# Two post-norm scale columns turned into rows: through a line of DRAM instead of diagonals on TensorE

## The reference, cut to what matters

```python
c_act = silu(c)
mod = c_act @ ada_w + ada_b                      # 6 vectors of 2048
sh1, sc1, g1, sh2, sc2, g2 = split(mod, 6)
u = rms_norm(x, mix_norm_pre) * (1 + sc1) + sh1
y = token_mixer(u)                               # retention and MoBA branches, gated, merged, @ w_out
x = x + (1 + g1) * rms_norm(y, mix_norm_post)    # first scale row
u = rms_norm(x, ffn_norm_pre) * (1 + sc2) + sh2
y = conv_ffn(u)                                  # @ w_up, causal conv, silu gate, @ w_down
x = x + (1 + g2) * rms_norm(y, ffn_norm_post)    # second scale row
```

## Time and profile before

| what | value |
|---|---|
| runs of the kernel | 1826.56, 1824.75, 1826.43 us (median 1826.43) |
| the profiled execution | 1826.54 us, span in the profile 1824.5 us |
| PE busy | 1804.5 us (99%) |
| VectorE busy | 1369.1 us (75%) |
| ScalarE busy | 859.4 us (47%) |
| granted TensorE clock | 0.997 of full speed |
| chain that ended last | PE 95%, DMA 2%, DVE 2%, ACT 1% |

### The profile page before, as it was taken

One profiled execution on the slowest core, in us unless ns is written; L12 is line 12 of the kernel. 1 busy time (PEld: TensorE's weight loads), 2 busy tenths in 40 slices (PEclk: granted clock), 3 DMA queues, 4 the chain that ended last, 5 costly groups with the idle time before them and its releaser, 6 DMA issues.

```text
span 1824.5 us, 26219 instructions
## 1 busy us (share of the span) xinstructions
PE 1804.5 (99%) x8989; PEld 1532.7 (84%) x8989; DVE 1369.1 (75%) x1968; ACT 859.4 (47%) x994; POOL 192.1 (11%) x271
## 2 busy tenths in 40 slices
PE   8999999999999999999999999999999999999998
PEld 6788888888888888888888888888888888888886
DVE  6887788878888788888997577777777776744555
ACT  4444544444454535463445455444444444444444
POOL 0000122222222222222210000000000000000000
PEclk9999999999999999999999999999999999999999
DMA  9999688878888888979886636556555555555552
GB/s 354 387 387 353 196 270 266 290 238 271 270 262 273 262 281 242 292 235 303 279 269 216 212 125 199 185 187 193 193 186 184 186 192 193 187 187 201 187 194 106
DMA packets 304739, 432.96 MB, mean 237 GB/s; under 512 B 50740, under 2 KB 174308, under 8 KB 304032
## 3 DMA queue, kind: packets, MB, share of 16 engines
q1 hardware_dynamic: 244160, 360.25, 59.7%
q0 software_dynamic: 20736, 67.34, 10.6%
q10 hardware_dynamic: 39776, 4.49, 1.8%
HBM read 429.79 MB, written 2.23 MB: 237 GB/s over the span
## 4 chain that ended last, share of the span: by engine, by line
PE 95%; DMA 2%; DVE 2%; ACT 1%; SPq 0%; issue 0%; DVEq 0%; ACTq 0%
PE ps L957 18%; PE ps L580 12%; PE ps L578 12%; PE ps L579 12%; PE ps L609 10%; PE ps L965 9%; PE ps L1026 4%; PE ps L1024 4%; PE ps L1025 4%; PE ps L711 1%; PE ps L713 1%; PE ps L712 1%; DMA ada_first<-in_ada_w 1%; PE ps L617 1%; DMA stage<-in_w_in 1%; DVE ada_acc L1600 1%
## 5 line engine op out<-in xcount | busy, mean ns | idle before, releaser
L1502 DVE TENSOR_TENSOR w_low<-stage,w_high 128x1024 fp32r<-128x1024 f32 x608 | 743.2, 1223 | 379.5 <-ACT w_high L1070 361.9
L1070 ACT ACTIVATE w_high<-stage 128x1024 fp32r<-128x1024 f32 x552 | 583.9, 1060 | 724.1 <-PE ps L580 274.0
L578 PE MATMUL ps<-w_high,lhs 128*128 128x512 f32 x992 | 389.4, 393 | 0.9 <-issue 0.9
L580 PE MATMUL ps<-w_high,lhs 128*128 128x512 f32 x992 | 386.3, 389 | 0.0
L579 PE MATMUL ps<-w_low,lhs 128*128 128x512 f32 x992 | 386.1, 389 | 0.0
L957 PE MATMUL ps<-lhs,w_high 128*128 128x512 f32 x1408 | 336.7, 391 | 0.0
L957 PEld LDWEIGHTS ps<-lhs,w_high 128*128 128x128 f32 x1408 | 258.5, 188 | 50.1 <-issue 0.2
L558 POOL DMA_DIRECT2D ada_ring<-in_ada_w x256 | 185.0, 723 | 753.8 <-DVE ada_acc L1526 544.4
L1526 DVE SCALAR_TENSOR_TENSOR ada_acc<-ada_ring,c_act,ada_acc 128x256 f32<-128x256 f32 x480 | 230.6, 480 | 20.9 <-DMA ada_ring<-in_ada_w 11.0
L578 PEld LDWEIGHTS ps<-w_high,lhs 128*128 128x128 f32 x992 | 186.2, 188 | 39.5 <-issue 1.3
L580 PEld LDWEIGHTS ps<-w_high,lhs 128*128 128x128 f32 x992 | 186.2, 188 | 39.0
(11 more groups left out here) (218 smaller groups left out, 1541.9 us busy)
## 6 DMA issues: line engine op xcount, KB each, us to landing
stage<-in_w_in SPq DMA_DIRECT2D x100, 1024.0 KB, 6.9
stage<-in_ffn_w_up SPq DMA_DIRECT2D x176, 512.0 KB, 4.4
ada_ring<-in_ada_w POOLq DMA_DIRECT2D x256, 256.0 KB, 5.7
stage<-in_ffn_w_down SPq DMA_DIRECT2D x44, 1024.0 KB, 5.0
ada_first<-in_ada_w SPq DMA_DIRECT2D x64, 512.0 KB, 11.4
stage<-in_w_in SPq DMA_DIRECT2D x56, 512.0 KB, 11.5
stage<-in_ret_w_o SPq DMA_DIRECT2D x16, 1024.0 KB, 6.8
stage<-in_moba_w_o SPq DMA_DIRECT2D x16, 1024.0 KB, 7.4
```

The lines of the kernel that those rows point to most:

```text
L578: pe.matmul(acc, hi, w_high[:, slot, k, :], start=kt == 0, stop=False)
L580: last = pe.matmul(acc, lo, w_high[:, slot, k, :], start=False, stop=kt == KT - 1)
L1070: act.activation(w_high[:, h % 4, :, :], stage[:, slot, 2 * (h % 2):2 * (h % 2) + 2, :], ACT.Copy).then_inc(high_ready, 1)
L1502: dve.tensor_tensor(w_low[:, h % 4, :, :], stage[:, slot, 2 * (h % 2):2 * (h % 2) + 2, :], w_high[:, h % 4, :, :].bitcast(F32), ALU.subtra ...
```

## The change

Both vectors take the same way. VectorE still works out the column (`gain_sum`, then one half of `gain`, now 128 x 2 x 16); the high and low parts, the diagonals, the spreads and the copies out of PSUM are gone. ScalarE writes the column with a DMA to a line of DRAM in feature order (`gain_to_memory`: 128 x 16 pieces of 4 bytes) and later, behind a wait on that write, issues a load that reads the 8 KB line 128 times into `gain_b` (`gain_to_rows`, 1 MB). First vector: write behind part 6 of the first G_MOBAO group, load behind part 2 of the second. Second vector: write behind part 6 of the third G_OUT group, load behind part 0 of the second up group. The idle matmuls read `ones_r[:, 0:1]` with a step of zero instead of `diag2`. PE's waits on `gain_ready` and `gain_diag` go; where the second spread waited for the modulated halves, the next up group's first part now does.

```diff
             def keep_busy(times):
                 for _ in range(times):
-                    pe.matmul(ps[:, 0, :], ones_r[:, :], diag2[:, 0:NC], start=True, stop=True)
+                    pe.matmul(ps[:, 0, :], ones_r[:, :], ones_r[:, 0:1].broadcast_to([P, NC]), start=True, stop=True)
...
                         elif first:
-                            pe.wait_ge(gain_ready, 5)
+                            pe.wait_ge(u2_even, KT // 2)
+                            pe.wait_ge(u2_odd, KT // 2)
...
-                    if G_MOBAO <= G < G_OUT and h == 5:
-                        spread_gain(G - G_MOBAO)
...
-                    if first and parity == 0 and h == 6:
-                        pe.wait_ge(u2_even, KT // 2)
-                        pe.wait_ge(u2_odd, KT // 2)
-                        pe.wait_ge(gain_diag, 4 * KT)
-                        for n in range(4):
-                            last = spread(4 + n, diag2, n)
-                        last.then_inc(gain_spread, 1)
...
+            def gain_to_memory(which):
+                act.wait_ge(gain_col, 2 * which + 2)
+                act.dma_start(gain_line[int(which)].rearrange("(k p) -> p k", p=P), gain[:, int(which), :],
+                              allow_slow_non_contiguous=True).then_inc(gain_out, 16)
+            def gain_to_rows(which):
+                act.wait_ge(gain_out, 16 * which + 16)
+                act.dma_start(gain_b[:, :], gain_line[which:which + 1, :].broadcast_to([P, D])).then_inc(gain_ready, 16)
...
-                    if G_MOBAO < G <= G_OUT and h == 1:
-                        k = G - 1 - G_MOBAO
-                        act.wait_ge(gain_spread, k + 1)
-                        act.activation(gain_b[:, k * NC:(k + 1) * NC], ps[:, 6, :], ACT.Copy).then_inc(gain_ready, 1)
+                    if (G, h) in ((G_MOBAO, 6), (G_OUT + 2, 6)):
+                        gain_to_memory(G > G_MOBAO)
+                    if G == G_MOBAO + 1 and h == 2:
+                        act.wait_ge(lhs_ready, 8 * 2 + 8)
+                        gain_to_rows(0)
...
                 if h == 0:
-                    act.wait_ge(gain_spread, 5)
-                    act.activation(gain_b[:, :].rearrange("p (b n) -> p b n", b=4), ps[:, 4:8, :], ACT.Copy
-                                   ).then_inc(gain_ready, 1)
+                    act.wait_ge(y_gained, 8)
+                    gain_to_rows(1)
...
-                    if G_MOBAO <= G < G_OUT and h == 5:
-                        k = G - G_MOBAO
-                        wait(dve, gain_spread, k - 1)
-                        for i in range(4):
-                            diagonal(diag1, k % 2, i, 4 * k + i)
...
                     if G > G_OUT and h == 3:
-                        dve.wait_ge(gain_ready, G - G_OUT)
+                        dve.wait_ge(gain_ready, 16)
...
-                    if G > G_OUT and h == 5:
-                        if G == G_OUT + 1:
-                            dve.wait_ge(gain_spread, 4)
-                            gain_column(1)
-                        k = G - 1 - G_OUT
-                        for i in range(16 * k // 3, 16 * (k + 1) // 3):
-                            diagonal(diag2, i // 4, i % 4, i)
+                    if G == G_OUT + 1 and h == 5:
+                        gain_column(1)
...
-            dve.wait_ge(gain_ready, 5)
+            dve.wait_ge(gain_ready, 32)
```

More of the change, by code:

```diff
@@ L134, in hybrid_block @@
         shift2 = sb("shift2", [P, KT])
-        gain = sb("gain", [P, KT])
-        gain_high = sb("gain_high", [P, KT], F32R)
-        gain_low = sb("gain_low", [P, KT], F32R)
+        gain_sum = sb("gain_sum", [P, KT])
+        gain = sb("gain", [P, 2, KT])
         post_cols = sb("post_cols", [P, 4 * KT])
@@ L167, in hybrid_block @@
                [("v_ret", [P, T, 1024], F32), ("o_ret", [P, T, 1024], F32)],
-               [("src_b", [P, KT, SEQ], F32)],
-               [("below_diag1", [P, KT // 2, SEQ], F32), ("diag1", [P, 4 * NC], F32R)])
+               [("src_b", [P, KT, SEQ], F32)])
         region("hold_r", 4096, [("src_a", [P, KT, SEQ], F32)])
@@ L297, in hybrid_block @@
         gain_col = sem("gain_col")
-        gain_diag = sem("gain_diag")
-        gain_spread = sem("gain_spread")
+        gain_out = sem("gain_out")
         gain_ready = sem("gain_ready")
@@ L333, in hybrid_block @@
         ada_line = nc.dram_tensor("ada_line", (4, ADA_BG), F32, kind="Internal").ap()
+        gain_line = nc.dram_tensor("gain_line", (2, D), F32, kind="Internal").ap()
         block = ctx.enter_context(nc.Block())
@@ L1823, in gain_column @@
                 a = (0, 3 * KT)[which]
-                dve.scalar_tensor_tensor(out=gain[:, :], in0=ada_cols[:, a:a + KT], scalar=1.0,
+                dve.scalar_tensor_tensor(out=gain_sum[:, :], in0=ada_cols[:, a:a + KT], scalar=1.0,
                                          in1=post_cols[:, (2 + which) * KT:(3 + which) * KT], op0=ALU.add, op1=ALU.add
                                          ).then_inc(gain_col, 1)
-                dve.wait_ge(gain_col, 4 * which + 1)
-                dve.tensor_tensor(gain[:, :], gain[:, :], post_cols[:, which * KT:(which + 1) * KT], ALU.mult
+                dve.wait_ge(gain_col, 2 * which + 1)
+                dve.tensor_tensor(gain[:, which, :], gain_sum[:, :], post_cols[:, which * KT:(which + 1) * KT], ALU.mult
                                   ).then_inc(gain_col, 1)
-                dve.wait_ge(gain_col, 4 * which + 2)
-                dve.tensor_copy(gain_high[:, :], gain[:, :]).then_inc(gain_col, 1)
-                dve.wait_ge(gain_col, 4 * which + 3)
-                dve.tensor_tensor(gain_low[:, :], gain[:, :], gain_high[:, :].bitcast(F32), ALU.subtract
-                                  ).then_inc(gain_col, 1)
-                dve.wait_ge(gain_col, 4 * which + 4)
-            def diagonal(diag, n, i, tile):
-                for part, column in enumerate((gain_high, gain_low)):
-                    at = (2 * n + part) * NC + i * P
-                    dve.tensor_scalar(diag[:, at:at + P], ident[:, :], column[:, tile:tile + 1].bitcast(F32), None,
-                                      ALU.mult).then_inc(gain_diag, 1)
             for G in range(G_RETO, G_UP):
@@ L1975, in first_up_side @@
                     mean_of_rows(slice(0, T), 3, 1)
-                    dve.wait_ge(gain_ready, 4)
+                    dve.wait_ge(gain_ready, 16)
                     gain_y(3, 0, 1)
```

7 lines of the change are left out of this document (1 added, 6 removed).

## The result

The changed kernel took 1830.94 us (median of 8 runs, 1828.23 to 1833.84), the kernel before 1826.49 us (8 runs, 1824.75 to 1827.26). The ratio is 1.003 with a 95% interval of 1.0021 to 1.0038: slower by 0.3%, where 0.2% faster was forecast and the range ended at 1825.6 us. The profiled execution took 1830.11 us; its span is 3.6 us longer than before's, and the medians are 4.45 us apart.

The account below looks back on a forecast made before the run. PE was taken to bound the kernel, busy 1804.5 of 1824.5 us. Removed PE work of 2.08 + 1.85 = 3.93 us, all else 0, took the median 1826.43 to 1822.50 us; range 1820.9 to 1825.6 us.

Parts of the forecast that it names:

- the removed work on PE: Spread matmuls gone from PE: four pairs in the MoBA output product, 2.08 us, plus eight later, 1.85 us; 3.93 us less.
- the second row's block: Eight spread matmuls between parts 6 and 7 of the first up group; removing them saves PE 1.85 us.
- no price for the edits on VectorE and ScalarE: Diagonal writes and copies removed, DMA issues added; both engines run ahead of PE, so 0 us.
- the loads of the rows: 1 MB broadcast loads on ScalarE's queue, 3.5 us each at 301 GB/s, within PE's 4.7 us slack; cost 0.
- the idle matmuls: 28 in the handover to the up projection, reading with step zero; equal slots of 0.23 us assumed, cost 0.
- the moved waits: Waits for the modulated halves, moved to the next up group's head; already met by then, no PE wait.
- Rival 2: Handover: zero-step read doubles the idle matmuls' slots, 5.4 us in all; net +1.5, 1827.9 us; chance 0.05.
- rival 3: Removed slots come back: weight stream or ada ring late once, 1 MB load up to 3.5 us; net -0.4; chance 0.07.
- I take 9 us, the slowest such row, within the 17.2: First column's write of 2048 4-byte pieces lands in 9 us, as the slowest ada_quads read; cost 0.
- The upper bound of 36 us: Column write's latest landing, if all of the slowest read grows with the pieces: 4 x 9.0 us.
- rival 1: First column's write lands after 17.2 us, ScalarE's load wait delays PE; at 36 us net +14.9, 1841 us; chance 0.08.
- the budget of 17.2 us: Time for the first column's write to land before PE waits for a low part: from 904.2 to 921.4 us.

Follow-up runs that it names:

- Dense: Changed kernel with each column written to DRAM as 128 pieces of 64 bytes, rows in another number order; 1822.15 us, ratio 0.9981 to the kernel before.
- zerostep: Kernel before with only the 28 idle matmuls' operand changed to one column of ones read with step zero; 1826.71 us, ratio 1.0002.
- Block: Dense with ScalarE, before the first load of the rows, also waiting until PE has finished part 2 of that group; 1830.27 us, ratio 1.0023.
- lateload: Changed kernel with the first load of the rows, and ScalarE's wait for the write, one group later, write unmoved; 1825.88 us, ratio 0.9999.

## Why the prediction was wrong

**Right: the removed work on PE.** The sum was 3.93 us. Dense and before differ by 3.97; the periods of the transposes after are 22.65 and 22.66 us where 22.64 was written, and the second row's block is worth 1.84 (1.85). The reading of slots from a period, ripple included, held.

**Right: no price for the edits on VectorE and ScalarE, the loads of the rows, the idle matmuls and the moved waits.** Dense has all of these edits and gains the whole sum; zerostep has the operand alone and costs nothing; and PE's waits after show none for the moved waits. Rival 2 falls. Of rival 3 the 1 MB load falls; its other half, an ada ring that is late once, did come, but through the write.

**Wrong: "I take 9 us, the slowest such row, within the 17.2".** The step was the landing of the write, and it measured 19.8 us. The row it was taken from had reads of 4-byte cells and writes of 32 bytes. I treated both as like a 4-byte write, on the ground that 512 pieces land no later than 128. What decided was none of these: with the same 2048 pieces 64 bytes apart the write lands in 14.0 us, inside the budget, and side by side in 19.8. The upper bound of 36 us covered it, but rival 1 got a chance of 0.08, although the number of pieces, the queue and the nearly full DMA engines stood there as grounds; a net price of 5.9 to 14.9 us against a gain of 4 asked for more, and the range should have reached it.

**Wrong: the budget of 17.2 us.** I went from the waiting instruction to ScalarE's and VectorE's next parts, and from those to the PE part that uses them. But between part 2 and part 3 stand the transposes on PE, and they need gate_a, which VectorE does behind the low part of part 3. The trace of before holds it, between the low part of 918.67 and the transposes of 925.37:

```profile
920.20 1.27 DVE L1863 TENSOR_TENSOR gate_b<-gate_b,ps 128x512 f32<-128x512 f32 x2
921.51 1.23 DVE L1866 TENSOR_TENSOR gate_a<-gate_a,gate_b 128x1024 f32<-128x1024 f32 x1
```

By the chain above the way from ScalarE's release to the transposes takes 5.6 us (924.91 to 930.52), so the latest moment was 925.37 - 0.5 - 5.6 = 919.3, 15.1 us after the issue and not 17.2. With this budget the landing of 19.8 us costs 4.7 us, and 4.85 were measured; by mine it would be 2.6. Block, which was given such a wait without the small write, bears the path out.

**Not foreseen: two further ways.** The write slowed the traffic beside it, a price that the prediction put at nothing and that stands even when nobody waits for the landing (lateload, 3.7 us). And the waits of 3.7 and 5.7 us were followed by a spell at the lower clock (1.83 us after, 2.08 in block). Rival 1 was priced as a wait alone. The whole: 1822.5 + 4.85 + 1.83 = 1829.2 us, within the changed kernel's runs but 1.8 us under their median. These runs spread more than those of before (5.6 us against 2.5), and one trace does not show what the longer ones had in addition.

By the Trainium skill's DMA: Bandwidth & Descriptors (Specifications) a transfer under 512 B is a read-modify-write. That pointed at the right instruction. The prediction made 18 us of it against a budget of 17.2; it came to 19.8 against 15.1. But no run here shows a read-modify-write as such, and the pieces of 64 bytes in dense are under that size as well and land in 3.1 to 4.4 us, so a size under 512 B did not by itself make a write late here.

## What to carry to other kernels

Do not write a column to DRAM in 4-byte cells side by side beside a stream that has no slack: turn it first, or write what a partition holds in one piece, or keep it for a time at which every stream has slack. When a wait is added, follow each engine's order to the first instruction of the bounding engine that is released through it, also if that belongs to other work; it may come before the one with the same number. And a rival whose price is larger than the gain belongs in the range even at a small chance.

## What the runs showed of the hardware

- 2048 writes of 4 bytes to neighbouring cells of DRAM took 14.3 to 19.9 us and cut the traffic beside them to about half (168 against 327 GB/s in dense over the same window); 256 of them took 11.9 us; 64 bytes apart 2048 took 8.0 to 14.0 us, beside 301 GB/s. Why neighbours hinder each other the runs don't show.
- Moving every later tile by 64 bytes in SBUF made the down projection's matmuls start 233.3 ns apart instead of 226.7 (859 against 884 matmuls in 200 us), 7 us in all. Elsewhere the pace stayed (1152 matmuls from 1300 to 1500 us in both). Of these matmuls' operands only `g_lhs` is moved; `w_high`, `w_low` and `lhs`, which the large products elsewhere read, are allocated ahead of the unused tile. That points to `g_lhs`, but no run moved it alone.
- Twenty idle matmuls that read one column with a step of zero took 4.53 us, against 4.83 with a diagonal of 512 columns.
- With PE waits of 3.7 us (after) and 5.7 us (block) the granted clock fell to its lower level, for 3.4 and 6.8 us by the windows (block: 0.94, 0.50 and 0.71 from 924 to 936 us). In block it fell within the wait (0.76 from 927 to 928 us, the wait ended at 930.5), in the changed kernel behind it (0.76 from 931 to 932 us). In lateload, with waits of 2.0 and 0.8 us, it stayed at 1.00. The period after the wait lost 1.83 us in the changed kernel and 2.08 in block.
